# A sixteen-expert layer in fp32: the down product as three products of high and low parts, interleaved with the next expert's turns

## What is computed

```python
for e in range(N_EXPERTS):                       # 16
    g, u = jnp.split(x @ w_gate_up[e], 2, axis=-1)   # w_gate_up[e]: 1024 x 512
    y = y + gate[:, e:e + 1] * ((jax.nn.silu(g) * u) @ w_down[e])   # w_down[e]: 256 x 1024
```

## Time and profile before

| | us |
|---|---|
| median of three runs (1736.61 to 1740.39) | 1738.0 |
| the profiled execution: its own time | 1743.86 |
| its span, first to last instruction | 1742.1 |
| TensorE busy with matmuls | 1546.2 (89%) |
| VectorE busy | 843.9 (48%) |
| ScalarE busy | 513.8 (29%) |
| GpSimd busy | 437.9 (25%) |

### The profile page before, as it was taken

How to read it: one execution, slowest core, us unless ns; L and a number is a source line. 1 busy time by engine, 2 the same in 40 slices (tenths; PEclk the granted TensorE clock), 3 DMA queues, 4 the chain that set the end, 5 groups by cost and what they waited for, 6 DMA issues and landing times.

```text
span 1742.1 us, 24604 instructions
## 1 busy us (share of the span) xinstructions
PE 1546.2 (89%) x9886; PEld 1349.0 (77%) x9886; DVE 843.9 (48%) x1547; ACT 513.8 (29%) x945; POOL 437.9 (25%) x460
## 2 busy tenths in 40 slices
PE   5979999999999998989999998999980999999910
PEld 5977579999997666789898988999970777777700
DVE  4026809999996775322464555442461111111127
ACT  3234531211112664400555554110120311111125
POOL 1744425623330000023333332331103000000055
PEclk8999999999998999999999999999995899999965
DMA  5111011223225503643111111252036487677445
GB/s 181 35 30 28 24 43 46 77 89 92 89 91 160 170 25 122 218 129 93 42 39 37 41 46 58 97 196 91 1 145 232 158 256 256 221 260 251 157 152 192
DMA packets 137798, 203.39 MB, mean 117 GB/s; under 512 B 14868, under 2 KB 89108, under 8 KB 137696
## 3 DMA queue, kind: packets, MB, share of 16 engines
q1 hardware_dynamic: 132512, 183.09, 33.1%
q0 software_dynamic: 5184, 18.88, 3.1%
HBM read 148.61 MB, written 53.33 MB: 116 GB/s over the span
## 4 chain that ended last, share of the span: by engine, by line
PE 84%; POOL 5%; DVE 4%; DMA 3%; ACT 2%; issue 2%; SPq 0%; POOLq 0%; ACTq 0%; DVEq 0%
PE psum L520 17%; PE psum L521 16%; PE psum L522 16%; PE psum L1258 10%; PE psum L1279 6%; PE psum L1089 3%; PE psum L1079 2%; PE psum L1111 2%; PE psum L962 2%; PE psum L1060 2%; PE psum L1175 1%; PE psum L1250 1%; POOL gathered_expert_out L897 1%; POOL y L902 1%; POOL x_by_expert L885 1%
## 5 line engine op out<-in xcount | busy, mean ns | idle before, releaser
L520 PE MATMUL psum<-x_hi,ring_hi 128*128 128x384 f32 x768 | 259.0, 337 | 0.5 <-ACT v L1433 0.5
L522 PE MATMUL psum<-x_lo,ring_hi 128*128 128x384 f32 x768 | 256.5, 334 | 0.0
L521 PE MATMUL psum<-x_hi,ring_lo 128*128 128x384 f32 x768 | 256.5, 334 | 0.0
L855 POOL CAST ring_hi<-ring_raw 128x512 fp32r<-128x512 f32 x88 | 66.9, 760 | 613.8 <-PE psum L522 380.2
L520 PE MATMUL psum<-w_hi,x_hi 128*128 128x256 f32 x576 | 175.2, 304 | 6.3 <-DVE channel_vectors L1692 3.7
L1258 PEld LDWEIGHTS psum<-expert_rows_T,w_gate_up 128*128 128x128 f32 x1024 | 170.1, 193 | 8.5 <-issue 8.5
L1258 PE MATMUL psum<-expert_rows_T,w_gate_up 128*128 128x192 f32 x1024 | 171.9, 330 | 0.7 <-ACT expert_rows_T L1617 0.7
L521 PE MATMUL psum<-w_hi,x_lo 128*128 128x256 f32 x576 | 166.5, 289 | 0.0
L522 PE MATMUL psum<-w_lo,x_hi 128*128 128x256 f32 x576 | 166.2, 288 | 0.0
L520 PEld LDWEIGHTS psum<-x_hi,ring_hi 128*128 128x128 f32 x768 | 144.2, 188 | 1.7 <-ACT v L1433 0.7
L521 PEld LDWEIGHTS psum<-x_hi,ring_lo 128*128 128x128 f32 x768 | 144.2, 188 | 1.1
(11 more groups left out here) (317 smaller groups left out, 3042.4 us busy)
## 6 DMA issues: line engine op xcount, KB each, us to landing
w_gate_up<-in_w_gate_up SPq DMA_DIRECT2D x16, 2048.0 KB, 9.0
ring_raw<-in_w_in SPq DMA_DIRECT2D x64, 256.0 KB, 3.4
w_down<-in_w_down SPq DMA_DIRECT2D x16, 1024.0 KB, 6.4
x_by_expert<-zeros SPq DMA_DIRECT2D x32, 384.0 KB, 5.3
expert_rows<-x_by_expert SPq DMA_DIRECT2D x16, 768.0 KB, 11.1
y_by_expert<-expert_out SPq DMA_DIRECT2D x16, 768.0 KB, 7.5
gate_sigmoid<-sigmoid_out SPq DMA_DIRECT2D x15, 576.0 KB, 3.2
w_raw<-in_w_in SPq DMA_DIRECT2D x16, 512.0 KB, 4.2
```

The lines of the kernel that those rows point to most:

```text
L520: nc.tensor.matmul(out, ah, bh, start=first, stop=False)
L521: nc.tensor.matmul(out, al, bh, start=False, stop=False)
L522: return nc.tensor.matmul(out, ah, bl, start=False, stop=last)
L855: link(g.tensor_copy(RHI[:, p_ % 2, :, :], RRAW[:, p_ % 2, :, :]))
```

## The change

The down product becomes three products of high and low parts. New tiles `WDH`, `WDL` (the down weights' parts) and `HEH`, `HEL` (those of the hidden values) exist once each, not twice. ScalarE makes both high parts, VectorE both low parts. The down product of expert e is moved behind the first half of the gate and up product of expert e+1, and its four products j alternate there with the four steps q of a turn. SyncE's queue is put in another order. Three semaphores of the router and one of the convolution are merged into others with the counts adapted; the instructions and waits there are the same.

```diff
+    WDH = sb("w_down_hi", [128, 2, D], XHo + 16384, f32r)
+    WDL = sb("w_down_lo", [128, 2, D], XHo + 24576, f32r)
+    HEH = sb("expert_hidden_hi", [128, 2, MS], XHo + 32768, f32r)
+    HEL = sb("expert_hidden_lo", [128, 2, MS], XHo + 34304, f32r)
...
 # SyncE
+            def expert_dma(i, par):
+                e = 2 * i + par
+                if not isinstance(e, int) or e + 3 < E:
+                    sp.wait_ge(s_expert_rows_turned, 4 * e + 8)
+                    sp.dma_start(XG[:, 1 - par, :, :], of(XS_1, e + 3)).then_inc(s_expert_rows_loaded[1 - par], 16)
+                if not isinstance(e, int) or e > 0:
+                    sp.wait_ge(s_expert_out, 4 * e)
+                    sp.dma_start(of(YS_1, e - 1), YE[:, 1 - par, :, :]).then_inc(s_expert_out_kept[1 - par], 16)
+                if not isinstance(e, int) or e + 2 < E:
+                    sp.wait_ge(s_down_lo, e + 1)
+                    sp.dma_start(WD[par][:, :, :], of(WD_D, e + 2)).then_inc(s_down_loaded[par], 16)
                     sp.wait_ge(s_gate_up_products, e + 1)
                     sp.dma_start(WG[par][:, :, :], of(WG_D, e + 2)).then_inc(s_gate_up_loaded[par], 16)
...
 # TensorE, in expert_products
                     if m == 1:
                         last.then_inc(s_gate_products, 1)
-                last.then_inc(s_gate_up_products, 1)
-                if not last_one:
-                    turn(i + par, 1 - par)
...
+                        for q in range(4):
+                            if not last_one:
+                                turn(i + par, 1 - par, q)
+                            if not isinstance(e, int) or e > 0:
+                                down_products(e - 1, q)
+                    if m == 3:
+                        last.then_inc(s_gate_up_products, 1)
+
+            def down_products(e, j):
+                if j == 0:
+                    pe.wait_ge(s_down_lo, e + 1)
+                    pe.wait_ge(s_hidden_lo, e + 1)
+                wait(pe, s_expert_out, 4 * e + j - 1)
+                h, nn = divmod(j, 2)
+                rows, cols = slice(MR * h, MR * h + MR), slice(512 * nn, 512 * nn + 512)
+                for k in range(2):
+                    last = mm3(PS[0:MR, 6 + j % 2, :], HEH[:, k, rows], HEL[:, k, rows], WDH[:, k, cols],
+                               WDL[:, k, cols], k == 0, k == 1)
+                last.then_inc(s_down_products, 1)
...
 # ScalarE, in expert_silu, after the turned rows of e + 1
+                act.wait_ge(s_down_loaded[par], 16 * i + 16)
+                wait(act, s_down_products, 4 * e)
+                a_(WDH[:, :, :], WD[par][:, :, :], ACT.Copy).then_inc(s_down_hi, 1)
+                act.wait_ge(s_hidden_ready, e + 1)
+                a_(HEH[:, :, :], HE[:, par, :, :], ACT.Copy).then_inc(s_hidden_hi, 1)
...
 # VectorE, in expert_hidden
+                if not isinstance(e, int) or e > 0:
+                    expert_out(i - 1 + par, 1 - par)
+                dve.wait_ge(s_down_hi, e + 1)
+                v.tensor_tensor(WDL[:, :, :], WD[par][:, :, :], WDH[:, :, :].bitcast(f32), ALU.subtract).then_inc(s_down_lo, 1)
                 dve.wait_ge(s_gate_up_products, e + 1)
                 dve.wait_ge(s_silu, e + 1)
-                wait(dve, s_down_products, 4 * e - 4)
                 v.tensor_tensor(HE[:, par, :, :], PS[:, 2 * par + 1, 0:2 * MS].rearrange("p (k n) -> p k n", k=2),
                                 SE[:, par, :, :], ALU.mult).then_inc(s_hidden_ready, 1)
+                dve.wait_ge(s_hidden_hi, e + 1)
+                v.tensor_tensor(HEL[:, :, :], HE[:, par, :, :], HEH[:, :, :].bitcast(f32), ALU.subtract).then_inc(s_hidden_lo, 1)
```

More of the change, by code:

```diff
@@ L758, in _ @@
                 sp.dma_start(XG[:, e, :, :], XS_1[e]).then_inc(s_expert_rows_loaded[e], 16)
-            def expert_dma(i, par, last):
+            def expert_dma(i, par):
                 e = 2 * i + par
-                if not last:
+                if not isinstance(e, int) or e + 3 < E:
[7 more added lines that the diff above has]
+                    sp.dma_start(WD[par][:, :, :], of(WD_D, e + 2)).then_inc(s_down_loaded[par], 16)
                     sp.wait_ge(s_gate_up_products, e + 1)
                     sp.dma_start(WG[par][:, :, :], of(WG_D, e + 2)).then_inc(s_gate_up_loaded[par], 16)
[L766 to L777, removed]
+            sp.wait_ge(s_expert_rows_turned, 4)
+            sp.dma_start(XG[:, 0, :, :], of(XS_1, 2)).then_inc(s_expert_rows_loaded[0], 16)
+            expert_dma(0, 0)
+            expert_dma(0, 1)
+            with sp.Fori(1, E // 2 - 2) as i:
+                expert_dma(i, 0)
+                expert_dma(i, 1)
+            for i in (E // 2 - 2, E // 2 - 1):
+                expert_dma(i, 0)
+                expert_dma(i, 1)
+            sp.wait_ge(s_expert_out, 4 * E)
+            sp.dma_start(of(YS_1, E - 1), YE[:, 1, :, :]).then_inc(s_expert_out_kept[1], 16)
             for i in range(2):
@@ L1233, in _, with turn @@
             router(TT - 1)
-            pe.wait_ge(s_choices_ready, 1)
+            pe.wait_ge(s_route_steps, 3)
             mm(PS[:, 5, 0:TT * E], BEFORE[:, :], G16[:, 5, :, :].rearrange("p t e -> p (t e)"), start=True, stop=False)
             mm(PS[:, 5, 0:TT * E], ONES[:, :], G16[:, 6, :, :].rearrange("p t e -> p (t e)"), start=False, stop=True)
-            mm(PS[:, 5, TT * E:TT * E + E], ONES[:, :], G16[:, 7, 0, :], start=True, stop=True).then_inc(s_positions_ready, 1)
-            def turn(i, par):
+            mm(PS[:, 5, TT * E:TT * E + E], ONES[:, :], G16[:, 7, 0, :], start=True, stop=True).then_inc(s_route_replies, 1)
+            def turn(i, par, q):
                 e = 2 * i + par
[L1244 to L1252, removed]
+                if q == 0:
+                    pe.wait_ge(s_expert_rows_loaded[par], 16 * i + 16)
+                wait(pe, s_expert_rows_stored, 4 * e + q - 1)
+                for k in range(2):
+                    for h in range(2):
+                        c = MS * k + MR * h
+                        last = tr(PS[:, 4 + q % 2, c:c + MR],
+                                  XG[:, par, h, 128 * (2 * q + k):128 * (2 * q + k) + 128], IDENT[0:MR, 0:MR])
+                last.then_inc(s_expert_rows_turned, 1)
             def gate_up(wg, xgt, bank):
@@ L1269, in expert_products @@
                         last.then_inc(s_gate_products, 1)
-                last.then_inc(s_gate_up_products, 1)
-                if not last_one:
-                    turn(i + par, 1 - par)
[L1273 to L1281, removed]
+                        for q in range(4):
[12 more added lines that the diff above has]
+                rows, cols = slice(MR * h, MR * h + MR), slice(512 * nn, 512 * nn + 512)
+                for k in range(2):
+                    last = mm3(PS[0:MR, 6 + j % 2, :], HEH[:, k, rows], HEL[:, k, rows], WDH[:, k, cols],
+                               WDL[:, k, cols], k == 0, k == 1)
+                last.then_inc(s_down_products, 1)
             pe.wait_ge(s_slot, 1)
-            turn(0, 0)
+            for q in range(4):
+                turn(0, 0, q)
             expert_products(0, 0)
@@ L1291, in _ @@
             expert_products(E // 2 - 1, 1, True)
+            for j in range(4):
+                down_products(E - 1, j)
             pe.wait_ge(s_expert_out, 4 * E)
```

47 lines of the change are left out of this document (25 added, 22 removed).

## The result

The changed kernel takes 1711.43 us (median of four, 1710.21 to 1717.5) beside 1738.6 before (now a median of four runs): a ratio of 0.9856, 95% interval 0.9838 to 0.9873, so 27.2 us less. A second set on another occasion gave 1710.54 beside 1738.36, ratio 0.9845 (0.9832 to 0.9859). The forecast was 1709.0, with 28.9 us of gain.

What follows compares the result with a forecast made beforehand. TensorE was taken to bound the experts, transfers next. Gains of 22.9 and 8.0 less 0.8 and 1.2 make 28.9 us: profiled 1743.9 becomes 1715.0, and 5.9 lower at the median, 1709.0 us; range 1703 to 1721.

Steps and rivals of the forecast that it cites:

- The down product: Experts' down product: 24 fp32r matmuls of 0.2267 us take 5.44 us, 1.43 less per expert, 22.9 us for 16.
- The wait in the turn: TensorE's wait for ScalarE's copy between groups of transposes goes: 0.575 us per expert, 8.0 us in 14 experts.
- the changes of kind: Eight switches per expert between fp32 and fp32r work on TensorE: 0.06 us lost per expert, 0.8 us in all.
- The parts: ScalarE makes WDH in 1.92 us and HEH in 0.51, VectorE WDL in 2.27 and HEL in 0.56, all hidden.
- Their cover: TensorE's gate and up product and turn hide the making of the parts, 3 us to spare; without it 1.2 per expert.
- The end: Last expert has no cover: TensorE's wait ahead of its down product, 0.79 us, grows by 1.2 us.
- SyncE's queue: Gate and up weights are needed 17.2 us after their request and land in 11 to 13: no cost, share 0.84.
- Changes that cost: Rival: each of eight switches between fp32 and fp32r work costs 0.11 us, 12.6 instead of 0.8: 1720.8 us, chance 0.10.
- Transfers that bind: Rival: the experts' transfers with gaps between batches set a period of 18.0 us, losing 11.2 us: 1720.2, chance 0.09.
- Two passes: Rival: each 512-column fp32r matmul of the down product takes 0.427 us, slower by 48 us: 1786, chance 0.03.
- a rate of 0.173 at 512 columns: Rival: down product's wide matmuls start every 0.173 us, saving 20.5 us more: 1688.5 us, chance 0.02.

Runs made afterwards that it cites:

- e8: Changed kernel with two of four down products at 128 stationary by 512 moving columns, two at 96 by 384, results not the layer's: 1700.51 us, single execution.
- e2: Kernel before, with the plain fp32 down product moved to the new place between the turn's steps, no parts made: 1729.09 us beside 1737.35, ratio 0.9959.
- e7: Changed kernel with two turn steps then two down products alternating, four changes of kind per expert instead of eight: 1709.52 us beside 1738.36, ratio 0.9845.
- e3: Changed kernel with one more VectorE subtraction per expert, directly ahead of the low part of the down weights: 1709.52 us beside 1737.35, ratio 0.9853.
- e1: Kernel before, with the down product in three products of parts but left in its old place, transfers in the old order: 1731.91 us beside 1737.35, ratio 0.9971.
- e5: The changed kernel measured again, unaltered, as the second set: 1710.54 us beside 1738.36, ratio 0.9845.
- e6: Changed kernel with one more load of 1024 KB per expert, behind the gate and up weights in SyncE's queue: 1712.05 us beside 1738.36, ratio 0.9851.
- e4: Changed kernel with each gate and up matmul in the experts replaced by three fp32r matmuls, results not the layer's: 1714.99 us beside 1737.35, ratio 0.9874.

## Why the prediction was right

**The down product.** 5.44 us were forecast from 24 x 0.2267; it takes 24 x 0.231 = 5.54, the mean of its starts in the trace of the change. One column per cycle held to within 0.002 us over 128 columns (e8); the forecast was short by 0.004 us per product, in all 1.6 us over 16 experts. This makes up the difference between 28.9 and 27.5. Where the 0.004 come from is open. About 0.001 goes with the narrow stationary (0.231 at 96 columns, 0.230 at 128), and at 384 moving columns the excess is 0.0015 instead of 0.003 to 0.004; nothing but these widths was tried. That a stationary of 72 columns also gives 0.173 us is not to be read from the earlier trace rows, but it is in the trace (starts at 90.46 and 92.02, nine matmuls apart). The 0.216 that the Trainium skill (TensorE: Matmul & The Clock Gate, Back-to-back issue gap) gives for 512 columns would have been further off than 0.2267.

**The wait in the turn.** Forecast 8.0 us less 0.8 for the changes of kind, 7.2 together. The period outside both products went from 1.875 to 17.287 - 10.40 - 5.54 = 1.35, which is 0.53 x 14 = 7.4 us. e2 shows the wait alone with 0.54 per expert, 7.6 us: the forecast took transposes at 0.080 us from start to start, and they take 0.083. The changes of kind, by e7 under 0.004 us each, cost at most 0.03 per expert, 0.4 us, and not 0.8. So the mechanism was right, but that the sum fits so well is in part luck: both terms were some 0.4 us too large, and they have opposite signs.

**The parts.** 1.92, 2.27, 0.51 and 0.56 us were read off other shapes by their slopes; measured were 1.91, 2.29, 0.52 and 0.56. Their cover held, with 3.6 us instead of the 3 forecast, and e3 shows that it is real. The prediction put what the cover is worth at 1.2 us per expert. e1, where the cover is gone and the chain of the hidden values overlaps the turn, lost 0.8.

**The end.** 1.2 us were forecast on top of 0.79, 1.05 came. **SyncE's queue** cost nothing, as forecast, though by a wrong size: the gate and up weights land in 9.9 us and not 11 to 13, the share became 0.79 and not 0.84. The base of that sum, 0.76, holds for 13 experts of the kernel before as well, so it is not the fault: the same bytes kept the engines busy 14.5 us per expert then and 13.7 now. Executions of the changed kernel differ too, with 0.81 in e5, so this figure tells little to the second digit. Rows took 11.3 us to land before and 5.2 now.

**The rivals.** Changes that cost are out by e7. Their price came from a wrong reading: the 0.11 us in the earlier trace rows lie inside the second group of transposes, which follows a wait. In the trace before, the first matmul of a down product starts 0.082 us after the last transpose, as one transpose after another does. Two passes and a rate of 0.173 at 512 columns are out by the product's 0.23, and so is the 0.131 that the Trainium skill (TensorE: Matmul & The Clock Gate, Back-to-back issue gap) gives as sustained: the measurement decides. Transfers that bind were a fair case, but the price I gave counted gaps between batches as lost time. The change has one such gap per expert, it is there because the next rows are requested only when TensorE has turned the last ones, and it closes under the extra load (e6); before e6 I still believed in it.

## What to carry to other kernels

Three fp32r products of parts beat one fp32 matmul only when the moving operand is wide: here 3 x 0.231 against 0.859 us at 512 columns, but 3 x 0.111 against 0.325 at 192. The parts bring a serial chain over two other engines between the value and its use, and the step pays in full only if independent TensorE work of that length stands in between: here the two edits gave 5.4 and 8.3 us alone and 27.2 together, so neither should be judged alone. A wait for a copy out of PSUM that recurs in every turn goes away when work of another kind is put between the steps; changing kinds cost under 0.004 us each time.

## What the runs showed of the hardware

- At a granted clock of 1.00, fp32r matmuls with 128 columns of stationary start every 0.111 us at 192 moving columns (e4), 0.120 at 256 and 0.173 at 384 (before), and 0.230 at 512 (e8): going from 256 to 192 columns saves 0.009 us, where the columns alone would save 0.027. Narrower ones were not measured.
- TensorE changed between fp32 transposes and blocks of six fp32r products eight times per expert and lost under 0.004 us per change (change against e7).
- The DMA engines moved 331 GB/s at a share of 0.96 over 225 us, and TensorE waited for no load in that time (e6). The gate and up weights took 10.1 us to land, against 9.9 without the extra load.
